# Sliding-window attention in a fused layer pair: a new order of ScalarE's and VectorE's steps, and the scaling of the probabilities by their inverse sums on GpSimd

## The reference, cut to what matters

```python
    scores = jnp.einsum('bnqhgd,bnkhd->bnhgqk', qb, kb) * scale
    scores = jnp.where(valid, scores, NEG_INF)
    m = jnp.maximum(jnp.max(scores, axis=-1, keepdims=True), sink)
    p = jnp.exp(scores - m)
    p = p / (jnp.sum(p, axis=-1, keepdims=True) + jnp.exp(sink - m))
    out = jnp.einsum('bnhgqk,bnkhd->bnqhgd', p, vb)
```

## Time and profile before

| what | value |
|---|---|
| median of 3 runs | 2418.4 us (2416.87 to 2419.04) |
| profiled execution: its time | 2417.04 us |
| profiled execution: its span | 2415.3 us |
| busy share PE / DVE / ACT / POOL | 98% / 63% / 41% / 6% |
| granted clock of TensorE | 0.999 of full speed |
| the attention's units in the span | about 164 to 522 us |

### The profile page before, as it was taken

How to read it: one execution, slowest core, us unless ns; L and a number is a source line. 1 busy time by engine, 2 the same in 40 slices (tenths; PEclk the granted TensorE clock), 3 DMA queues, 4 the chain that set the end, 5 groups by cost and what they waited for, 6 DMA issues and landing times.

```text
span 2415.3 us, 30564 instructions
## 1 busy us (share of the span) xinstructions
PE 2361.2 (98%) x11300; PEld 1957.8 (81%) x11300; DVE 1526.2 (63%) x2395; ACT 979.7 (41%) x1675; POOL 139.7 (6%) x189
## 2 busy tenths in 40 slices
PE   8999898999999999999999999999999999999998
PEld 6787777778888888888788888898888888888886
DVE  6746767656777764434654663374499888883335
ACT  6335555533344342223043243264354444442124
POOL 1000000011000010112000020012100000000000
PEclk9999999999999999999999999999999999999999
DMA  5112223235323243331111033263122222244313
GB/s 198 41 44 71 70 70 114 71 113 133 103 88 96 88 164 98 103 115 49 53 44 31 27 109 92 85 197 125 37 68 85 89 87 78 78 140 139 104 61 123
DMA packets 253361, 222.19 MB, mean 92 GB/s; under 512 B 7246, under 2 KB 225571, under 8 KB 252226
## 3 DMA queue, kind: packets, MB, share of 16 engines
q1 hardware_dynamic: 233920, 148.39, 20.2%
q0 software_dynamic: 15424, 56.53, 7.4%
q10 hardware_dynamic: 3906, 15.78, 2.0%
HBM read 171.39 MB, written 49.28 MB: 91 GB/s over the span
## 4 chain that ended last, share of the span: by engine, by line
PE 80%; DVE 11%; ACT 5%; issue 2%; DMA 1%; SPq 0%; ACTq 0%; DVEq 0%
PE bank L993 10%; PE bank L994 10%; PE bank L995 10%; PE bank L1589 4%; PE bank L1590 4%; PE bank L1591 4%; PE bank L1226 4%; PE bank L1228 4%; PE bank L1227 4%; DVE Sx L2820 2%; PE bank L1630 2%; PE bank L1632 2%; PE bank L1631 2%; ACT Sx L1878 2%; ACT q_hi_twice L1871 2%
## 5 line engine op out<-in xcount | busy, mean ns | idle before, releaser
L1705 ACT ACTIVATE whi<-wraw 128x1024 fp32r<-128x1024 f32 (+2 forms) x159 | 160.5, 1009 | 481.3 <-PE bank L995 263.6
L2624 DVE TENSOR_TENSOR wlo<-wraw,whi 128x1024 fp32r<-128x1024 f32 (+1 forms) x174 | 204.4, 1175 | 143.5 <-ACT whi L1705 137.5
L1176 PE MATMUL bank<-xhi,whi 128*128 128x512 f32 x384 | 149.6, 390 | 0.0
L1178 PE MATMUL bank<-xhi,wlo 128*128 128x512 f32 x384 | 149.6, 390 | 0.0
L1177 PE MATMUL bank<-xlo,whi 128*128 128x512 f32 x384 | 149.6, 390 | 0.0
L1878 ACT ACTIVATE Sx<-Sx,small 128x256 f32<-128x256 f32 x128 | 63.6, 498 | 158.8 <-DVE small L2826 158.8
L993 PE MATMUL bank<-x2hi,whi 128*128 128x512 f32 x240 | 93.9, 391 | 0.0
L994 PE MATMUL bank<-x2lo,whi 128*128 128x512 f32 x240 | 93.4, 389 | 0.0
L995 PE MATMUL bank<-x2hi,wlo 128*128 128x512 f32 x240 | 93.4, 389 | 0.0
L1630 PE MATMUL bank<-ffn_hi,whi 128*128 128x512 f32 x240 | 93.4, 389 | 0.0
L1631 PE MATMUL bank<-ffn_lo,whi 128*128 128x512 f32 x240 | 93.4, 389 | 0.0
(11 more groups left out here) (529 smaller groups left out, 6620.3 us busy)
## 6 DMA issues: line engine op xcount, KB each, us to landing
wraw<-in_w_in_dram SPq DMA_DIRECT2D x85, 512.0 KB, 3.9
wraw<-in_ffn_w_up_dram SPq DMA_DIRECT2D x44, 512.0 KB, 3.8
filler_spill<-filler POOLq DMA_DIRECT2D x24, 512.0 KB, 3.2
ffn_spill<-ffn_value SPq DMA_DIRECT2D x22, 512.0 KB, 3.4
gate<-filler_spill POOLq DMA_DIRECT2D x16, 512.0 KB, 3.9
wraw<-in_xattn_wkv_dram SPq DMA_DIRECT2D x16, 512.0 KB, 3.9
wraw<-in_ffn_w_down_dram SPq DMA_DIRECT2D x16, 512.0 KB, 3.7
ffn_raw<-ffn_spill ACTq DMA_DIRECT2D x14, 512.0 KB, 4.6
```

The source lines that it names most:

```text
L1176: pe.matmul(ps(m % 3), whi[slot][:, k, :], xh, start=(k == 0), stop=False)
L1178: last = pe.matmul(ps(m % 3), wlo[slot][:, k, :], xh, start=False, stop=(k == KT - 1))
L1705: act.activation(whi[slot][:, 0:n, 0:m], wraw[slot][:, 0:n, 0:m], ACT.Copy).then_inc(s_whi, 1)
L2624: dve.tensor_tensor(wlo[slot][:, 0:n, :], wraw[slot][:, 0:n, :], whi[slot][:, 0:n, :].bitcast(F32), ALU.subtract).then_inc(s_wlo, 1)
```

## The change

Four things are changed, all in the attention's units.

`normalise` keeps the denominator and the reciprocal on VectorE; the four multiplications of `Sx` move to GpSimd (`scale_probs`), behind a new semaphore `s_den`. ScalarE's unit u now is `unit_hi(u)`, `turned_hi(u-2)`, `exps(u-1)`, `keep_o(u-3)`, splits, where it was splits, `unit_hi(u)`, `turned_hi(u-2)`, `keep_o(u-3)`, `exps(u)`. VectorE's unit u now begins with `load_rq(u-1)` and `maxima(u-1)`, then `turned_lo(u-2)`, `unit_lo(u)`, the late half tile of the unit before, the rest of `normalise(u-1)`, `sum_o(u-3)`, and last the splits and the early half tile. TensorE's order is the same.

```diff
+            def scale_probs(u):
+
+                par = u % 2
+                pool.wait_ge(s_den, u + 1)
+                for hh in range(4):
+                    last = pool.tensor_scalar(Sx[par][:, hh, :], Sx[par][:, hh, :], den[par][:, hh:hh + 1], None,
+                                              ALU.mult)
+                last.then_inc(s_p, 1)
+
             for u in range(UNITS):
+                if u:
+                    scale_probs(u - 1)
                 for m in range(1, 2 * FILL_IN, 2):
                     if HALVES_DONE[m][0] == u:
                         store_filler(m // 2)
...
+            scale_probs(UNITS - 1)
             load_x_again(1)
...
             for u in range(UNITS):
                 if u == 0:
                     split(T_F + 1, (T_F + 1) % 2)
-                splits_due(u, False)
                 unit_hi(u)
+                if u >= 2:
+                    turned_hi(u - 2)
+                if u >= 1:
+                    exps(u - 1, (u - 1) % 2)
                 if u == 0:
                     q_sum(1)
-                if u >= 2:
-                    turned_hi(u - 2)
+                if u == 1:
+                    query_root(1)
                 if u >= 3:
                     keep_o(u - 3)
+                splits_due(u, False)
                 splits_due(u, True)
-                exps(u, u % 2)
-                if u == 1:
-                    query_root(1)
...
             def normalise(u, par):
                 dve.wait_ge(s_exp, u + 1)
                 order.link(dve.tensor_tensor(den[par][:, :], sums[par][:, :], es[par][:, :], ALU.add))
-                order.link(dve.reciprocal(den[par][:, :], den[par][:, :]))
-                for hh in range(4):
-                    last = dve.tensor_scalar(Sx[par][:, hh, :], Sx[par][:, hh, :], den[par][:, hh:hh + 1], None,
-                                             ALU.mult)
-                last.then_inc(s_p, 1)
+                dve.reciprocal(den[par][:, :], den[par][:, :]).then_inc(s_den, 1)
...
             for u in range(UNITS):
                 if u == 0:
                     split(T_F + 1, (T_F + 1) % 2)
-                splits_due(u, False)
-                unit_lo(u)
+                if u >= 1:
+                    load_rq(u - 1)
+                    maxima(u - 1)
+                if u == 2:
+                    query_inverse(1)
+                if u >= 2:
+                    turned_lo(u - 2)
+                unit_lo(u)
                 if u >= 1:
+                    halves_due(u - 1, False)
                     normalise(u - 1, (u - 1) % 2)
-                if u >= 2:
-                    turned_lo(u - 2)
+                if u == 1:
+                    query_var(1)
                 if u >= 3:
                     sum_o(u - 3)
-                if u == 1:
-                    query_var(1)
+                splits_due(u, False)
                 halves_due(u, True)
                 splits_due(u, True)
-                load_rq(u)
-                maxima(u)
-                halves_due(u, False)
-                if u == 1:
-                    query_inverse(1)
```

More of the change, by code:

```diff
@@ L436, in hybrid_then_mixer_kernel @@
         s_exp = sem("exp_done")
+        s_den = sem("denominators_ready")
         s_p = sem("probs_ready")
@@ L1904, in _ @@
                     split(T_F + 1, (T_F + 1) % 2)
-                splits_due(u, False)
                 unit_hi(u)
+                if u >= 2:
+                    turned_hi(u - 2)
+                if u >= 1:
+                    exps(u - 1, (u - 1) % 2)
                 if u == 0:
                     q_sum(1)
-                if u >= 2:
-                    turned_hi(u - 2)
+                if u == 1:
+                    query_root(1)
                 if u >= 3:
                     keep_o(u - 3)
+                splits_due(u, False)
                 splits_due(u, True)
-                exps(u, u % 2)
-                if u == 1:
-                    query_root(1)
             t = T_F + FILL_IN
+            turned_hi(UNITS - 2)
+            exps(UNITS - 1, (UNITS - 1) % 2)
             splits_due(UNITS, False)
-            turned_hi(UNITS - 2)
             keep_o(UNITS - 3)
@@ L2871, in _ @@
                     split(T_F + 1, (T_F + 1) % 2)
-                splits_due(u, False)
+                if u >= 1:
[5 more added lines that the diff above has]
+                    turned_lo(u - 2)
                 unit_lo(u)
                 if u >= 1:
+                    halves_due(u - 1, False)
                     normalise(u - 1, (u - 1) % 2)
-                if u >= 2:
-                    turned_lo(u - 2)
+                if u == 1:
+                    query_var(1)
                 if u >= 3:
                     sum_o(u - 3)
-                if u == 1:
-                    query_var(1)
+                splits_due(u, False)
                 halves_due(u, True)
                 splits_due(u, True)
-                load_rq(u)
-                maxima(u)
-                halves_due(u, False)
-                if u == 1:
-                    query_inverse(1)
-            t = T_F + FILL_IN
+            t = T_F + FILL_IN
+            load_rq(UNITS - 1)
+            maxima(UNITS - 1)
+            halves_due(UNITS - 1, False)
+            turned_lo(UNITS - 2)
+            normalise(UNITS - 1, (UNITS - 1) % 2)
             splits_due(UNITS, False)
-            normalise(UNITS - 1, (UNITS - 1) % 2)
-            turned_lo(UNITS - 2)
             sum_o(UNITS - 3)
```

## The result

The kernel after takes 2400.19 us (median of 4 runs, 2399.61 to 2401.74), the kernel before beside it 2418.69 us (4 runs, 2416.87 to 2419.04): a ratio of 0.9925, 95% interval 0.9913 to 0.9938. It is faster by 18.5 us. Faster was forecast, but by 38 us, and 2400.2 lies above the range's end of 2397.

What follows compares the result with a forecast made beforehand. TensorE was taken as the bound, waiting on VectorE's order in the attention's units. Removing 39.0 us of waits less about 1 us gave 2418.4 - 38 = 2380.4 us; range 2376.5 to 2397.

Steps and rivals of the forecast that it cites:

- I take 0.42, because only one tensor streams: Scalings on GpSimd: 0.42 us each, four in 1.7 us, probabilities ready at 7.5, or 8.0 behind a DMA.
- 0.40 and 0.77 as its ends: Bounds for one GpSimd scaling: 0.40 us from an in-place select, 0.77 from a two-tensor addition with some fixed time.
- The break-even: Longest GpSimd scaling that still stays hidden before the next turn: 0.95 us, or 0.82 behind a DMA.
- the first rival: GpSimd's scalings late in part of the units, at 0.75 to 1.0 us or port-blocked: 2386 to 2400; chance 0.16.
- The shared port: VectorE's split beside GpSimd's scalings in 19 units: hidden at 0.42 us a scaling, 15 us lost at 0.77 with full blocking.
- The DMA ahead: GpSimd's queue in 12 units after a late tile: store takes 0.55 us, scalings start at 6.3 instead of 5.8.
- A late half tile: VectorE's list, in 20 of the 32 units: takes 0.68 us, to 5.7 after the turn.
- The floor: TensorE's unit with no wait: 9.62 us against 10.92, so at most 39.0 us to win over thirty units.
- the 1 us left for the head of the phase: One remaining wait of about 1 us, where a square root stands on ScalarE between two sets of exponentials.
- the 33.4 of the waits: TensorE's waits put the gain at 33.4 us; 39.0 was explained by counting from 0.16 instead of 0.28 after a matmul's start.
- Both waits of the earlier trace: TensorE's waits for VectorE's `ptlo` (31.0 us) and `qlo` (2.4 us) were to be gone.
- The steps up to the reciprocal: After a turn: maxima done at 2.4, exponentials 3.1 to 5.3, `turned_lo` to 4.3, reciprocal at 5.7 or 6.1 us.

Runs made afterwards that it cites:

- e7: Kernel after, with GpSimd scaling only the first 128 of each head's 256 columns: 2382.85 us, 0.9854 of the kernel before.
- e12: Kernel after, with GpSimd copying each head's probabilities onto themselves instead of scaling them: 2376.78 us, 0.9827 of the kernel before.
- e1: Kernel after, with the four scalings back on VectorE behind the reciprocal, so the new order alone: 2375.36 us, 0.9822 of the kernel before.
- e11: Kernel after, with VectorE's weight split of the filler tiles doing only 16 of each 128 columns: 2388.81 us, 0.9876 of the kernel before.
- e2: Kernel before, in its old order, with only the four scalings moved to GpSimd: 2415.29 us, 0.9988 of the kernel before.
- e8: Kernel after, with VectorE's split in the units multiplying the raw weights by a constant instead of subtracting two inputs: 2398.36 us, 0.9918 of the kernel before.
- e4: Kernel after, with GpSimd's store of a late tile and the load of x issued behind the scalings: 2395.96 us, 0.9908 of the kernel before.
- e9: Kernel before, with the new order on ScalarE alone; VectorE keeps its old order and the scalings: 2400.44 us, 0.9927 of the kernel before.

## Why the prediction was wrong, step by step

**The step that failed: "I take 0.42, because only one tensor streams".** The scaling takes 0.91 us with nothing beside it (with e7's half width: 2.5 ns a column, 0.27 fixed; a copy has 0.4 in all, e12). The prediction kept 0.40 and 0.77 as its ends, and even the upper was too low: the fixed part stood in it with 0.13 us. With copies in the scalings' place the rest of the chain gave 2376.8, so it is this term that carried the error. The break-even worked out for it, 0.95 or 0.82 behind a DMA, was kept by 0.91 in a unit with nothing else, by less than 0.1 us (end at 9.50, turn due at 9.54 by e1, started at 9.61). It was missed behind a DMA, beside a split, and already behind a late half tile without a store: there the scalings start 260.08 - 253.86 = 6.22 after the turn, and the unit takes 9.92. The change went the way of the first rival, GpSimd late in part of the units, whose time ended at 2400.

**The shared port: what a split costs hung on the length of the scaling.** The prediction had a split cost nothing with 0.42, and up to 15 us with 0.77. It costs 11.4 us (e11, the clock's 1.6 among them), 0.50 to 0.65 us per group in 19 units. Within a group it is a single scaling that grows. In the kernel after, beside the split from 301.38 to 302.79:

```profile
302.14 1.44 POOL L876 TENSOR_SCALAR Sx<-Sx,small 128x256 f32<-128x256 f32 x1
```

and in e2:

```profile
202.36 2.40 POOL L876 TENSOR_SCALAR Sx<-Sx,small 128x256 f32<-128x256 f32 x1
...
202.75 1.21 DVE L2637 TENSOR_TENSOR wlo<-wraw,whi 128x1024 fp32r<-128x1024 f32 x1
```

The first starts 0.76 us behind the split's start, the second 0.39 ahead of it, and both end 0.8 us behind the split's end, as do all the scalings that a split holds up in these two kernels (0.78 to 0.80). So the one that is caught does nearly all of its 0.91 us behind the split. The groups of copies of e12 show that VectorE can pay too:

```profile
292.21 2.42 POOL L876 COPY Sx<-Sx 128x256 f32<-128x256 f32 x4
...
292.48 1.90 DVE L2638 TENSOR_TENSOR wlo<-wraw,whi 128x1024 fp32r<-128x1024 f32 x1 [0.25 <-ACT whi L1717]
```

GpSimd pays 2.42 - 1.43 = 0.99 us and VectorE 1.90 - 1.22 = 0.68. Beside the scalings it was 0.50 to 0.65 and up to 0.19. The Trainium skill, SBUF — State Buffer, § Who interferes with whom, says that the pair of ports which the two share is an exclusive lock: whoever issues first has it for its whole instruction, and the other blocks. The trace agrees on the block of the scaling that is caught, but not on the order, as far as the starts tell it: in e2 that scaling had started first, and the split beside it took its usual 1.21. The same section says that `tensor_scalar` on VectorE can enter a mode that takes both ports; e8, one input and a group longer by 0.37, fits that, though no view here shows the mode.

**The DMA ahead: 0.5 us reckoned, 0.8 measured.** The scalings start at 6.78 behind a store and at 5.96 without. VectorE's part of the unit at 294.43:

```profile
299.58 0.69 DVE L2647 TENSOR_TENSOR filler<-bank,R 128x512 f32<-128x512 f32 x1
300.38 0.18 DVE L2853 RECIPROCAL small<-small 128x4 f32<-128x4 f32 x1
```

The reciprocal is there at 300.56 - 294.43 = 6.13, as forecast for such a unit (6.1). The half tile is out at 300.27, but the issue begins at 300.57 only, and takes 0.60 (0.55 reckoned). That start 0.30 us behind the half tile's end (the same in all 12 such stores) is what the sum lacked, with 0.14 for a half tile that is out later than the 5.7 reckoned. Not all of the 0.8 is the store's: behind a late half tile alone the scalings start at 6.22, and with the store moved away in e4 at 6.21. The store itself is worth 0.57 us a unit. e4 got back 4.2 us by moving it and the load of x, net of what the splits then took back. A late half tile comes in 24 of the 32 units, not in 20 as the prediction has it; no term of its sum hangs on that.

**The floor.** A unit with no wait was read as 9.62, from a unit that itself began behind a wait. It is 9.54 behind a unit that had none (e1), where the transposes take 1.03 and not 1.06 to 1.09. Thirty units in e1 took 285.30 us (turn 0 at 180.85, turn 30 at 466.15; the first unit only 8.64), so the most to be won was 327.61 - 285.30 = 42.3, not 39.0; and the 1 us left for the head of the phase was not needed. The reason given for 39.0 lying above the 33.4 of the waits doesn't come out either: 0.12 us in each of 30 waits is 3.6, and the difference was 5.6.

**What was right.** Both waits of the earlier trace rows go with the new order, nearly the whole gain is carried to the end of the program (in e1 the last turn comes 42.5 us earlier and the span is 41.1 shorter, with no wait of TensorE over 0.5 us behind the units), and VectorE was never short of time: e1 leaves it the 1.14 us a unit of the scalings and is the fastest. The steps up to the reciprocal came within 0.2 us.

**Where the 24.8 us went.** Against e1's 9.54, the kernel after has 10 units with a DMA ahead and a split beside (10.75 to 11.89 us each, 14.1 us lost), 9 with a split alone (10.16 to 11.81, 8.0 us) and 11 with neither (9.60 to 9.92, 2.0 us): 24.1 us in all. The rest of the 24.97 us by which the thirty units are longer than e1's is that e1's first took 8.64 and not 9.54. The causes add within a unit, and so have no separate shares: without the splits 11.4 us come back, with the store behind 4.2, with half the columns 17.3, with two of the four heads 21.4.

The largest two units are one event. Unit 20's scalings stood behind a store and behind the load of x:

```profile
382.71 0.60 POOL L852 DMA_DIRECT2D filler_spill<-filler  x1 [6.20 <-DVE filler L2647]
383.30 0.92 POOL L869 DMA_DIRECT2D x_again<-x_spill  x1
384.26 4.14 POOL L876 TENSOR_SCALAR Sx<-Sx,small 128x256 f32<-128x256 f32 x4
```

TensorE waited 2.1 us for them. In the windows view (busy us of PE, PEld, DVE, ACT, POOL with counts, granted clock, DMA share, GB/s) the clock then is 0.51 of full speed, its level of 1.2 GHz:

```profile
388.45:391.90 3.45, 3.45 (x12) 3.08 (x13) 0.26 (x4) 0.00 (x0) 0.00 (x0) 0.51 0.99 342
...
400.26:402.10 1.84, 1.84 (x12) 1.69 (x13) 1.81 (x10) 0.00 (x0) 1.84 (x3) 1.00 1.09 360
```

The same 8 transposes and 4 matmuls took 3.45 us there and 1.84 in the next unit, so the stall cost 1.6 us more than its length. e4 and e11 both shorten this stall (their longest waits are 1.6 us), and neither has the half clock, so its 1.6 us are in what each of them brings.

**Left open.** What of the 0.27 us is a start and what the column of scalars; why the copies that start within a split run at their full speed and lengthen it, and only the last of them is held; what takes the 0.30 us ahead of a store; and whether the half clock comes with every idle of some 2 us: in e2 it did behind 2.34 and 2.25 us and not behind three of 2.2. In e8, behind 2.02, the 8 transposes took 1.66, and in e9, behind 1.60, once 1.55, where the other idles of that length there left them at 1.06.

## What to carry to other kernels

First ask which order the waiting engine's partners work in, and give the work back its old engine as a control: here the order was worth 43 us and the move of work cost 25. An operation is priced by its own row or by one of the same kind, not by one of the same number of inputs; if there is none, its distance to the break-even is part of the forecast, and so are the DMA issues ahead of it in the queue and the operations of VectorE beside it. Two lists that are tied by semaphores are changed together: one half alone can close a loop that is longer than the one it was to break.

## What the runs showed of the hardware

- GpSimd's multiplication by a column of scalars takes 0.91 us for 128x256 in fp32, 0.59 for 128x128, 0.83 with a constant; its copy of 128x256 takes 0.39 to 0.41. VectorE does four of the multiplications in 1.14 us where GpSimd takes 3.64. The Trainium skill, GPSIMD Engine Reference, § 4.1 Engine selection, calls GpSimd's operations with one input roughly at line rate: the copy agrees, the multiplication doesn't, even with a constant.
- VectorE's weight split (two inputs, 1.22 us) holds up one GpSimd multiplication beside it until 0.8 us behind its own end, also one that had started 0.39 us earlier (e2). A VectorE operation with a single input lengthens the group too (4.01 against 3.64 us).
- A store issued on GpSimd's queue begins 0.30 us behind the operation that it waits for and takes 0.60; the multiplications behind it start 0.57 us later for it.
- An idle of TensorE of 2.1 us was followed by 3.45 us at half clock; behind the other waits of the units in the same trace, 1.65 us and less, the 8 transposes kept their 1.06 to 1.10 us.
